# Three output projections regrouped: 256 rows of weights against four accumulator banks, the first chunk ahead of the last head's values

## The reference

```
x = x + moba_attention(h, w_q, w_o, ...)      # layer 1: 8 heads of 128, ends in  o @ w_o
x = x + mem_cross_attention(norm(x), norm(mem), w_q, w_kv, w_o)   # both layers: 4 heads of 256
def mem_cross_attention(h, mem_n, w_q, w_kv, w_o):
    ...
    p = softmax(s)
    o = einsum("bhsm,bmhd->bshd", p, v).reshape(bsz, seq, 1024)
    return o @ w_o                             # [256 x 1024] @ [1024 x 1024]
x = x + swiglu(norm(x), w_gu, w_down)
```

## Time and profile before

| | us |
|---|---|
| median of 3 runs | 1720.01 (1718.95 to 1724.0) |
| the profiled execution | 1721.94, of which the span is 1720.2 |
| PE busy | 1511.6 (88%) |
| DVE busy | 877.0 (51%) |
| ACT busy | 666.5 (39%) |
| mean granted TensorE clock | 0.945 of full speed |

### The profile page before, as it was taken

The page is one execution under the profiler, slowest core; times in us unless marked ns, Lnnn a source line. Parts: engine busy times, 40 slices in busy tenths (PEclk is TensorE's granted clock), DMA queues, the critical chain, the costliest instruction groups (busy, mean ns, idle before and its releaser), DMA issues.

```text
span 1720.2 us, 34148 instructions
## 1 busy us (share of the span) xinstructions
PE 1511.6 (88%) x14318; PEld 1313.3 (76%) x14318; DVE 877.0 (51%) x1234; ACT 666.5 (39%) x899; POOL 148.0 (9%) x189
## 2 busy tenths in 40 slices
PE   9999999999998999999999999899998656665657
PEld 8999999988998989998898899688974333333333
DVE  5876466645685755665676689866641000000001
ACT  5545455434445445443565745435442000000001
POOL 5900000000000000000106002130010000000000
PEclk9999999999999999999999999899999787887788
DMA  7765656774743766666455244002899999999996
GB/s 254 258 203 177 206 162 195 223 263 151 269 148 126 266 197 169 186 193 207 146 150 154 92 153 143 26 27 87 318 400 417 427 434 428 431 431 430 430 430 292
DMA packets 238193, 417.13 MB, mean 242 GB/s; under 512 B 13730, under 2 KB 213993, under 8 KB 228073
## 3 DMA queue, kind: packets, MB, share of 16 engines
q1 hardware_dynamic: 237881, 414.62, 66.9%
q10 hardware_dynamic: 176, 0.53, 0.1%
HBM read 414.07 MB, written 1.06 MB: 241 GB/s over the span
## 4 chain that ended last, share of the span: by engine, by line
PE 61%; issue 28%; ACT 5%; DVE 5%; DMA 1%; POOL 0%; SPq 0%; ACTq 0%; DVEq 0%; POOLq 0%
PE bank_sums L464 9%; PE bank_sums L466 9%; PE bank_sums L465 9%; PE bank_sums L480 3%; PE bank_sums L482 3%; PE bank_sums L481 3%; PE bank_sums L1174 2%; PE bank_sums L1175 2%; PE bank_sums L1176 2%; ACT w_hi L243 1%; PE bank L2021 1%; PE bank_sums L492 1%; PE bank_sums L494 1%; PE bank_sums L493 1%; PE bank_sums L2021 1%
## 5 line engine op out<-in xcount | busy, mean ns | idle before, releaser
L250 DVE TENSOR_TENSOR w_lo<-w_raw,w_hi 128x2048 fp32r<-128x2048 f32 (+2 forms) x177 | 399.9, 2262 | 225.7 <-ACT w_hi L243 221.9
L243 ACT ACTIVATE w_hi<-w_raw 128x2048 fp32r<-128x2048 f32 (+2 forms) x177 | 332.0, 1880 | 157.2 <-DMA w_raw<-in_ffn_w_down_dram 49.3
L464 PE MATMUL bank_sums<-h_hi,w_hi 128*128 128x256 f32 x1152 | 322.1, 280 | 5.9 <-DVE h_lo L674 3.0
L466 PE MATMUL bank_sums<-h_hi,w_lo 128*128 128x256 f32 x1152 | 321.1, 279 | 0.0
L465 PE MATMUL bank_sums<-h_lo,w_hi 128*128 128x256 f32 x1152 | 321.1, 279 | 0.0
L2903 PE MATMUL bank<-w_exp_four,xeT 128*32 128x256 f32 x1600 | 140.3, 523 | 112.1 <-DMA w_exp_four<-in_w_gate_dram 60.7
L464 PEld LDWEIGHTS bank_sums<-h_hi,w_hi 128*128 128x128 f32 x1152 | 218.2, 189 | 7.3 <-issue 6.8
L466 PEld LDWEIGHTS bank_sums<-h_hi,w_lo 128*128 128x128 f32 x1152 | 216.6, 188 | 0.0
L465 PEld LDWEIGHTS bank_sums<-h_lo,w_hi 128*128 128x128 f32 x1152 | 216.4, 188 | 0.0
L2903 PEld LDWEIGHTS bank<-w_exp_four,xeT 128*32 128x32 f32 x1600 | 69.4, 148 | 181.0 <-issue 113.8
L3066 DVE TENSOR_TENSOR hx<-sg,bank 128x256 f32<-128x256 f32 x16 | 6.8, 422 | 278.4 <-ACT sg L3036 278.4
(11 more groups left out here) (589 smaller groups left out, 3083.7 us busy)
## 6 DMA issues: line engine op xcount, KB each, us to landing
w_exp_four<-in_w_up_dram SPq DMA_DIRECT2D x13, 4096.0 KB, 33.5
w_exp_four<-in_w_down_dram SPq DMA_DIRECT2D x13, 4096.0 KB, 33.6
w_exp_four<-in_w_gate_dram SPq DMA_DIRECT2D x12, 4096.0 KB, 34.6
w_raw<-in_ffn_w_gu_dram SPq DMA_DIRECT2D x88, 512.0 KB, 5.1
w_raw<-in_w_in_dram SPq DMA_DIRECT2D x54, 512.0 KB, 4.9
w_mod<-in_w_mod_dram SPq DMA_DIRECT2D x24, 1024.0 KB, 8.2
w_raw<-in_ffn_w_down_dram SPq DMA_DIRECT2D x44, 512.0 KB, 4.5
w_raw<-in_mem_w_kv_dram SPq DMA_DIRECT2D x32, 512.0 KB, 4.5
```

The lines of the kernel that those rows point to most:

```text
L243: e.activation(whi[slot][:, 0:w], raw[slot][:, 0:w], ACT.Copy).then_inc(S["hi_ready"], 1)
L250: e.tensor_tensor(wlo[slot][:, 0:w], raw[slot][:, 0:w], whi[slot][:, 0:w].bitcast(F32), ALU.subtract).then_inc(S["lo_ready"], 1)
L464: e.matmul(dst, whi[slot][:, lo:hi_], bh[:, k, :], start=begin, stop=False)
L466: ins = e.matmul(dst, wlo[slot][:, lo:hi_], bh[:, k, :], start=False, stop=end)
```

## The change

Chunks of the three projections become 256 rows of weights over all columns, into the four banks at once, with 24 matmuls of 512 columns, as in `down`. The first chunk needs only the first head of the memory attention (the first two of the other). Its loads, its matmuls and one split are put into the queues at the last head, between `modulate_folded` and the values of that head; `modulate_folded` goes ahead of that piece. `rest` puts the three other chunks on PE, the three other splits on ACT and DVE, and behind them four adds of one bank each. The norm behind it gets the add of bank 3 as the wait for its second token tile (`half`). The next product begins in bank 2.

```diff
@@ attention, by_parts
-                next(parts, None)
                 if h == heads - 1:
                     modulate_folded(vector)
+                next(parts, None)
                 tl = values(h, tc)
@@
+    def followed(parts, idle, begin):
+        yield from parts
+        for _ in range(idle):
+            yield
+        begin()
+        yield
+    class OutProjection:
+        def __init__(self, W, held_bank):
+            self.rows = W.rearrange("(c k p) n -> p c k n", p=P, k=2)
+            self.first_order = sorted(DOWN_BANKS, key=lambda b: b in (3, held_bank))
...
+        def chunk(self, e, c):
+            slot = (self.base + c) % RING
+            e.wait_ge(S["hi_ready"], self.base + c + 1)
+            e.wait_ge(S["lo_ready"], RING + self.base + c + 1)
+            last = c == 3
+            banks = DOWN_BANKS if c else self.first_order
+            for kk, b in ([(kk, b) for b in banks for kk in range(2)] if last else
+                          [(kk, b) for kk in range(2) for b in banks]):
+                k, t_, hf = 2 * c + kk, b // 2, b % 2
+                if c == 0 and kk == 0:
+                    for w in self.free[b]:
+                        e.wait_ge(*w)
+                if b == banks[0]:
+                    e.wait_ge(*self.tiles[k])
...
+                e.matmul(G[b][:, :], fh, w0, start=(k == 0), stop=False)
+                e.matmul(G[b][:, :], fh, w1, start=False, stop=False)
+                ins = e.matmul(G[b][:, :], fl, w0, start=False, stop=(k == KT - 1))
+                if last and kk == 1 and b != banks[-1]:
+                    ins.then_inc(down_bank, 1)
+            ins.then_inc(S["chunk_used"], 1)
+        def split(self, c):
+            m = self.base + c + AHEAD
+            act.raw(lambda e: hi_split(e, m, m % RING))
+            dve.raw(lambda e: lo_split(e, m, m % RING))
+        def begin(self):
+            self.base = st.n
+            self.free = [list(w) for w in bank_free]
+            load_chunks(4, self.source, self.base)
+            st.n += 4
+            pe.raw(lambda e: self.chunk(e, 0))
+            self.split(0)
+        def rest(self):
+            for c in range(1, 4):
+                pe.raw(lambda e, c=c: self.chunk(e, c))
+            for c in range(1, 4):
+                self.split(c)
...
+            for i, b in enumerate(DOWN_BANKS):
+                t_, hf = b // 2, b % 2
+                xs = x[:, t_, hf * BANK:(hf + 1) * BANK]
+                tok = dve.do(lambda e, b=b, xs=xs: e.tensor_tensor(xs, xs, G[b][:, :], ALU.add), ...)
+                bank_free[b] = [tok]
+                if b == 3:
+                    half = [tok]
+            st.bank = DOWN_BANKS[0]
+            return tok, half
@@ the three places (memory attention shown)
-        to = attention(4, 2, ..., parts=last_queries, second=value_bank)
-        gemm(4, cols(A["mem_w_o"][l]), tm_chunk(a_hi, a_lo), dve_chunk=add_tm(x), ready=[to])
+        projected = OutProjection(A["mem_w_o"][l], value_bank)
+        attention(4, 2, ..., parts=followed(last_queries, 2, projected.begin), second=value_bank, tls=projected.tiles)
+        x_out = projected.rest()
```

More of the change, by code:

```diff
@@ L713, in split_biased, with norm_to_features @@
         return tls[-1]
-    def norm_to_features(src, ready, gain, free, vector=None):
-        rows = norm_rows(src, ready)
+    def norm_to_features(src, ready, gain, free, vector=None, half=None):
+        rows = norm_rows(src, ready, half)
         if vector is not None:
@@ L721, in norm_to_features, with attention @@
         return split_features(turn_rows(xn, rows), gain, free)
-    def attention(heads, kts, scale, score, v, pbuf, ptbuf, ready, vector=None, causal=None, free=(), parts=None, second=None, beside=None, behind=None, ahead=None):
+    def attention(heads, kts, scale, score, v, pbuf, ptbuf, ready, vector=None, causal=None, free=(), parts=None, second=None, beside=None, behind=None, ahead=None, tls=None):
         t_soft, t_pt, t_pv = {}, {}, {}
@@ L814, in values @@
             return tl
-        tls = []
+        tls = [] if tls is None else tls
         def by_parts():
@@ L1069, in mem_attention @@
+    def mem_attention(l, features, into, key, vector, x_ready, half=None):
         W = A["mem_w_kv"][l]
-        x_ready = dve_evacs()
-        rows = norm_rows(x, [x_ready])
+        rows = norm_rows(x, [x_ready], half)
         if l == 0:
@@ L1095, in mem_attention, with ffn @@
         value_bank = next(b for b in ((st.bank + 3) % RING, (st.bank + 2) % RING) if b != 3)
-        to = attention(4, 2, 256 ** -0.5, score, vv, (pb0, pb1), ptb,
-                       lambda h: [values_ready, (S["act_evac"], q_evacs - 2 + h)], free=[all_used()],
-                       vector=vector, parts=last_queries, second=value_bank)
-        gemm(4, cols(A["mem_w_o"][l]), tm_chunk(a_hi, a_lo), dve_chunk=add_tm(x), ready=[to])
+        projected = OutProjection(A["mem_w_o"][l], value_bank)
+        attention(4, 2, 256 ** -0.5, score, vv, (pb0, pb1), ptb,
+                  lambda h: [values_ready, (S["act_evac"], q_evacs - 2 + h)], free=[all_used()],
+                  vector=vector, parts=followed(last_queries, 2, projected.begin), second=value_bank, tls=projected.tiles)
+        x_out = projected.rest()
         for j in range(4):
             sp.raw(mod_load((2, 5)[l], j))
-    def ffn(l, between=None, after_bank=None):
-        tx = norm_to_features(x, [dve_evacs()], lambda k: col("norm_ffn", 8 * l + k), [all_used()], vector=(2, 5)[l])
+        return x_out
+    def ffn(l, x_in, between=None, after_bank=None):
+        tx = norm_to_features(x, [x_in[0]], lambda k: col("norm_ffn", 8 * l + k), [all_used()], vector=(2, 5)[l], half=x_in[1])
         W = A["ffn_w_gu"][l].rearrange("(k p) (h n) -> p k h n", p=P, h=2)
@@ L1145, in ffn @@
         return tok, half, extra
-    DOWN_BANKS = (2, 3, 0, 1)
-    down_bank = nc.alloc_semaphore("down_bank")
-    down_n = {"n": 0}
     def down(n, source, beside, held):
@@ L1226, in rope_fm @@
         return dve.do(lambda e: e.tensor_tensor(b3, b3, tmp[0:rows, 0:tiles, :], ALU.add), t)
-    mem_attention(0, h2, (h_hi, h_lo), lambda k: kT[:, k, :], 1)
-    tx, tx1, _ = ffn(0)
+    x_mem = mem_attention(0, h2, (h_hi, h_lo), lambda k: kT[:, k, :], 1, dve_evacs())
+    tx, tx1, _ = ffn(0, x_mem)
     rows = norm_rows(x, [tx], tx1)
@@ L1282, in score1 @@
         return e.matmul(dst, qT[:, h, t_ * P:(t_ + 1) * P], kT[:, h, 0:(t_ + 1) * P], start=True, stop=True)
[L1283 to L1286, removed]
+    projected = OutProjection(A["moba_w_o"][0], 3)
+    attention(8, 1, 128 ** -0.5, score1, vv, (pb0, pb1), ptb, [t_q, t1, t_causal],
+              causal=causal, free=[all_used()], vector=0, parts=followed(memory_side, 0, projected.begin), second=3,
+              tls=projected.tiles)
+    x_moba = projected.rest()
+    x_mem = mem_attention(1, (h_hi, h_lo), h2, lambda k: keys2[k // 6][:, k % 6, :], 4, *x_moba)
     A0 = sbuf_at["a_hi"]
     XN = sbuf_at["xn"]
-    mem_done = [all_used(), dve_evacs(), act_evacs()]
+    mem_done = [all_used(), dve_evacs(), act_evacs(), x_mem[0]]
     gt = place("gt", [P, 2, D], F32, offset=F0)
@@ L1380, in build @@
     vq, roots = small[:, 104:108], small[:, 108:112]
-    tx, tx1, tcol = ffn(1, modulation_rows, gained)
+    tx, tx1, tcol = ffn(1, x_mem, modulation_rows, gained)
     C_Z, C_B, C_CQ, C_CKV, C_KR, C_G = 3072, 4096, 4128, 4640, 4896, 4960
```

15 lines of the change are left out of this document (14 added, 1 removed).

## The result

| | before | after |
|---|---|---|
| median (16 runs each, same chip) | 1720.85 us (1712.9 to 1728.56) | 1726.38 us (1722.57 to 1732.57) |
| ratio, 95% interval | | 1.0035 (1.0021 to 1.005) |
| span of the profiled execution | 1720.2 us | 1724.1 us |
| mean granted clock | 0.945 | 0.944 |

What follows compares the result with a forecast made beforehand. The prediction took PE, with its waits at the projections' seams, to bound the first block; +1.5 and +1.2 us at the memory projections and +0.2 at layer 1's own gave 1722.9 us, range 1715.5 to 1727.5.

Steps and rivals of the forecast that it cites:

- What bounds the kernel: First block: PE sets the time, by its matmuls and the few waits, chiefly the seam behind each projection.
- part 3: Behind the projections: all four adds queue behind splits awaiting late landings; +1.5 and +1.2 us at memory seams, +0.2 third.
- The third seam: Behind layer 1's own attention: `mem_w_kv` matmuls wait for bank 2's add; +0.2 us, between -0.6 and +0.7.
- Parts 1 and 2: Projections on PE: 512-column matmuls, -0.6 us each; first chunk ahead of the last head's values, -0.2 per memory projection.
- Part 4: The rest, including bank numbering shifted by two after each `ffn`: taken as 0, with -1.2 to +1.2 us for the range.
- Rival C: Memory seams: the clock falls in new idle time, up to 1.7 us each, +6.3 in all, 1726.3 us; chance 0.17.
- Sum: Whole kernel: +1.5, +1.2 and +0.2 make +2.9 us, from a median of 1720.01 to 1722.9.
- the likeliest case: Whole kernel: the main forecast, adds held by splits, 1722.9 us, own range 1720.6 to 1725.3; chance 0.50.
- Rival D: Projections on PE: 512-column matmuls as dense as 256-column ones, -11.3 us each, about 1686 us; chance 0.01.

Runs made afterwards that it cites:

- e2: Changed kernel with two of the four modulation transfers issued behind feed-forward chunk 1 instead of ahead of those weights; ratio 1.0007 to the kernel before.
- e5: Changed kernel, bank numbering kept, `lo_split` of the next product's chunk 1 put behind the norm's row scaling in both memory projections; ratio 0.9964 to the kernel before.
- e1: Changed kernel without the line that lets the next product begin in bank 2 (numbering kept); ratio 1.0027 to the kernel before.
- e7: Changed kernel, bank numbering kept, with 22 matmuls that nothing reads on PE behind each memory projection; ratio 1.0015 to the kernel before.
- e8: Kernel before with only the third and fourth modulation transfer issued behind feed-forward chunk 1; ratio 0.9993 to the unedited kernel before.
- e6: Changed kernel, numbering kept, two modulation transfers later, first chunk behind the last head's values in all three projections; ratio 0.9999 to the kernel before.
- e3: Changed kernel with bank numbering kept and two of the four modulation transfers behind feed-forward chunk 1; ratio 0.9978 to the kernel before.
- e10: Kernel before with `lo_split` of the next product's chunk 1 behind the row scaling after both memory attentions; ratio 1.0024 to the unedited kernel before.
- e11: The same kernel as e5, timed once more in five rounds; ratio 0.999 to the kernel before.

## Why the prediction came out as it did

- **What bounds the kernel, and part 3**: right in place and mechanism. In both memory seams the adds stand back to back behind a `lo_split` whose chunk lands hardly earlier or not at all (21.84 us against 21.72 before in the first, 21.66 against 21.96 in the second), and e2 and e5 take the loss away from two sides. Size at full clock: +1.54 (e1) and +1.38 (e7) in the first seam against +1.5 forecast, and +1.36 (e7) in the second against +1.2. The path from the last add to the transposes, taken as 4.22, measured 4.22.
- **The third seam**, +0.2 forecast, +0.13 between the two profiles: right by luck. Both had lost the clock there, which lengthened the old form's seam by 1.6 us (31.18 against e8's 29.60), while the new form's stood where its landing puts it. Where the clock held, the changed form gave 29.4 to 30.9 against 29.60 at the same spacing of the matmuls, and 29.6 and 29.7 against 28.54 at the closer one; the term is nearer +1, because the form made a PE-bound seam hang on a landing that moves by 3 us from version to version. Why that landing moves is open.
- **Parts 1 and 2**: forecast -0.6 and -0.2 a seam, and on PE just that came out: its projection ends 25.42 us behind `modulate_folded` before, 24.79 in e6, 24.58 in e3 and in the kernel after. As said, they were inside the adds' delay and brought the memory seams nothing.
- **Part 4 is the term that was mis-sized**: taken as 0, it measured 1.27 + 1.03 us of waits (+1.35 and +1.14 in the stages). I wrote that no row prices it. None of the rows that I had read does, but the trace of the kernel before does: the bank order is in the code, and DVE lets go of the last gate/up chunk's bank at 346.61, a slack of 0.18 us ahead of the fourth bank's first matmul; at the second place it is at 777.48, 0.40 us ahead of 777.88. Moving that bank from the fourth place to the second takes 6 matmuls, 6 x 0.229 = 1.4 us, and 1.4 - 0.18 = 1.2 and 1.4 - 0.4 = 1.0 us is what it costs. I also looked to the wrong side of the kernel for it: I named the second block, where no length stands out from the scatter of 874.2 to 880.0 us, and the waits came in the first block's own `ffn`, where the evidence at the first place is the wait itself (its stage took 187.2 to 188.7 us in kernels with no such wait and the same spacing).
- **Rival C** did happen, in both memory seams, at a third of its price: 0.5 to 0.8 us each and not 1.7, since most of the lost PE time lay where PE waited anyway. The rule of the Trainium skill ("TensorE: Matmul & The Clock Gate", section "HAM oscillation") that gaps of idle PE let the next burst start cold agrees with the kernel after (2.76 and 2.58 us idle, clock 0.50 and 0.51) and with e7 (no idle, clock 1.00), and not with e1's first seam (2.52 us idle, clock 1.00). What the page describes is a wait for a DMA in every turn of a loop; these seams are single waits for another engine.
- **Sum**: +2.9 forecast, of it +2.7 at the memory seams, where +2.7 (e7) to +2.9 was measured at full clock; with about 1.1 to 1.3 of the clock, 2.5 of the numbering and 0.1 of the third seam that makes the 6.6 found. The forecast time, 1722.9, was 3.5 us below the median measured, 1726.4, which lies above the end of the likeliest case (1725.3) and close to rival C's 1726.3. That closeness is chance: C reckoned 3.4 us for the clock where it cost some 1.2, and nothing for the numbering, which cost 2.5.
- **Rival D** fell at once: 512-column matmuls stand 0.229 us apart in the new projections too.

## What to carry to other kernels

When adds move behind a queue of splits, ask what each split waits for: a split whose data lands late is best put behind everything that the path needs, and this was worth more here (31.75 to 28.90, 2.9 us a memory seam) than the regrouping itself (0.8). And read on past the end of the stretch that you measure: the split went ahead of the low features and took 0.4 of the 2.9 back there. When a change shifts which buffer the next stages use, find every place with a fixed order of buffers and compute the slack of the last reader; it can be done from the trace of the kernel before. And where totals scatter by 1%, measure the stretch between two instructions that both versions have.

## What the runs showed of the hardware

At a granted clock of 1.00, the 256-column matmuls of the gate/up chunks ran at one of two spacings, which did not change within a feed-forward stage. Two stretches of the kernel before, in its first and second feed-forward part:

```profile
300.19 0.28 PE L464 MATMUL bank_sums<-h_hi,w_hi 128*128 128x256 f32 x1
...
302.90 0.28 PE L464 MATMUL bank_sums<-h_hi,w_hi 128*128 128x256 f32 x1
...
700.31 0.28 PE L464 MATMUL bank_sums<-h_hi,w_hi 128*128 128x256 f32 x1
...
703.14 0.28 PE L464 MATMUL bank_sums<-h_hi,w_hi 128*128 128x256 f32 x1
```

That is 24 matmuls in 2.71 and in 2.83 us, 0.113 and 0.118 apart (0.1133 and 0.1178 as means over the stages). Over the 1056 matmuls of the 22 gate/up chunks it makes 4.7 us: the second stage took 187.8 us in e3, e6 and e8, and 192.4 to 192.5 in the kernel before, e1 and e7. The 240 matmuls of the third seam in the old form show it too (0.118 apart in e8, 0.113 in e10). It does not go with the kernel: e5 and e11 are the same code, and both stages ran at 0.113 in the one profile and at 0.118 in the other, whose spans are 1710.8 and 1719.6. The two stages differ by (193.43 - 188.73) + (192.83 - 188.16) = 9.4 us and so account for the whole 8.8 between the spans. That the total of e5 first looked twice as good as its seams fits this, though only the profiled runs show their spacing. What chooses the spacing is open.
